# The last tile's expert outputs: one load for both halves, summed by TensorE, and a norm that reads PSUM

## The reference

```python
def _rmsnorm(x, g):
    xf = x.astype(jnp.float32)
    y = xf * lax.rsqrt(jnp.mean(xf * xf, axis=-1, keepdims=True) + RMS_EPS)
    return (y * g.astype(jnp.float32)).astype(x.dtype)

    # in _hier_moe: every token gets the weighted outputs of its two experts
    for e in range(N_EXPERTS):
        hid = jax.nn.silu(t @ w_gate[e]) * (t @ w_up[e])
        out = out + combine[:, e:e + 1] * (hid @ w_down[e]).astype(jnp.float32)

    # in _layer and reference
    x = x + _hier_moe(_rmsnorm(x, g_ffn), ...)
    y_prompt = _rmsnorm(xp, g_final)
    y_sample = _rmsnorm(xs, g_final)
```

## Time and profile before

| What | Value |
|---|---|
| Time, median of 3 runs | 513.92 us (513.32 to 516.14) |
| Profiled execution | 512.16 us, its span 510.40 us |
| Mean granted clock of TensorE | 0.984 |
| Busy: TensorE, VectorE, ScalarE, GpSimd | 468.6, 295.2, 114.2, 206.4 us |
| DMA over the span | 141.35 MB, mean 277 GB/s |

### The profile page before, as it was taken

How to read it: one execution, slowest core, us unless ns; L and a number is a source line. 1 busy time by engine, 2 the same in 40 slices (tenths; PEclk the granted TensorE clock), 3 DMA queues, 4 the chain that set the end, 5 groups by cost and what they waited for, 6 DMA issues and landing times.

```text
span 510.4 us, 9147 instructions
## 1 busy us (share of the span) xinstructions
PE 468.6 (92%) x3279; PEld 279.5 (55%) x3280; DVE 295.2 (58%) x575; ACT 114.2 (22%) x231; POOL 206.4 (40%) x298
## 2 busy tenths in 40 slices
PE   6999999999999999999789989989978999897993
PEld 3887777777777734645454444434434444443431
DVE  4219999999999946556843233323223333332367
ACT  5130010110112332112422122212212211221243
POOL 3010914694769840011263443444434344434600
PEclk9989999999999999999799999999999999999997
DMA  8796004300000099869969999999999999999995
GB/s 326 245 378 149 1 3 171 158 1 0 1 0 1 1 308 414 310 223 327 401 257 412 382 399 405 411 367 412 409 405 408 409 415 410 413 403 410 400 335 198
DMA packets 47571, 141.35 MB, mean 277 GB/s; under 512 B 10338, under 2 KB 12402, under 8 KB 43435
## 3 DMA queue, kind: packets, MB, share of 16 engines
q1 hardware_dynamic: 41466, 128.80, 66.3%
q0 software_dynamic: 4960, 9.49, 5.0%
q10 hardware_dynamic: 1113, 2.62, 1.3%
HBM read 134.90 MB, written 13.19 MB: 290 GB/s over the span
## 4 chain that ended last, share of the span: by engine, by line
PE 71%; DMA 7%; SPq 7%; DVE 6%; POOL 3%; issue 3%; ACT 2%; DVEq 0%; ACTq 0%; POOLq 0%
PE banks L1557 26%; PE banks L1774 10%; PE banks L1794 9%; PE banks L1769 8%; PE banks L1615 8%; DMA region_x<-in_w_up 3%; DMA region_w<-in_w_in 3%; SPq L488 2%; SPq L494 2%; PE banks L1865 2%; PE banks L1784 2%; PE banks L1721 1%; DVE region_m L1431 1%; DVE region_m L1429 1%; PE banks L1645 1%
## 5 line engine op out<-in xcount | busy, mean ns | idle before, releaser
L1557 PE MATMUL banks<-region_m,region_w 128*128 128x256 f32 (+1 forms) x576 | 141.9, 410 | 0.0
L1557 PEld LDWEIGHTS banks<-region_m,region_w 128*128 128x128 f32 x576 | 110.7, 192 | 30.4 <-issue 0.4
L1418 DVE TENSOR_TENSOR region_m<-region_m,banks 128x512 f32<-128x512 f32 x30 | 20.6, 688 | 71.7 <-ACT region_m L787 71.7
L1089 DVE SCALAR_TENSOR_TENSOR z<-region_m,z 128x512 f32<-128x512 f32 x60 | 49.6, 826 | 0.0
L950 POOL COPY scol<-sidx 128x1 uint32 x28 | 13.4, 480 | 86.8 <-DVE region_m L1418 86.8
L1429 DVE TENSOR_TENSOR region_m<-region_m,banks 128x128 f32<-128x128 f32 x30 | 8.7, 288 | 65.5 <-ACT region_m L781 65.5
L1089 DVE SCALAR_TENSOR_TENSOR region_x<-region_m,region_x 128x512 f32<-128x512 f32 x56 | 45.5, 812 | 0.0
L863 POOL TENSOR_TENSOR region_m<-region_x 128x512 f32<-128x512 f32 x4 | 20.2, 5046 | 61.4 <-ACT region_m L666 30.8
L1794 PE MATMUL banks<-region_w,region_m 128*32 128x512 f32 x272 | 40.3, 598 | 2.8 <-DVE region_m L1431 2.8
L787 ACT ACTIVATE region_m<-banks,w_row 128x512 f32<-128x512 f32 x30 | 20.6, 687 | 97.6 <-PE banks L1794 97.6
L654 ACT ACTIVATE region_x<-banks 128x256 f32<-128x256 f32 (+1 forms) x40 | 14.2, 407 | 120.7 <-PE banks L1557 103.9
(11 more groups left out here) (265 smaller groups left out, 723.0 us busy)
## 6 DMA issues: line engine op xcount, KB each, us to landing
region_w<-in_w_down SPq DMA_DIRECT2D x16, 1024.0 KB, 16.0
region_w<-in_w_gate SPq DMA_DIRECT2D x12, 1024.0 KB, 13.1
region_w<-in_w_up SPq DMA_DIRECT2D x12, 1024.0 KB, 16.0
region_m<-in_w_down SPq DMA_DIRECT2D x12, 1024.0 KB, 17.6
region_w<-in_w_in SPq DMA_DIRECT2D x4, 2048.0 KB, 15.2
region_m<-in_w_gate SPq DMA_DIRECT2D x8, 1024.0 KB, 14.8
region_m<-in_w_up SPq DMA_DIRECT2D x8, 1024.0 KB, 17.2
region_w<-in_w_out SPq DMA_DIRECT2D x1, 4096.0 KB, 12.9
```

The costliest lines, as they stand in the source:

```text
L1089: last[j % 2] = conv(nc.vector.scalar_tensor_tensor(out=acc[j % 2], in0=ub[:, c, j:j + SEQ], scalar=wB(c, j), in1=acc[j % 2], op0=ALU.mult ...
L1418: nc.vector.tensor_tensor(yblk[b], yblk[b], held[b], ALU.add).then_inc(s_ya, 1)
L1557: ins = mm(ps[2 * bank + j][:, 0:LEN[j]], sec[name][:, k, c * P:(c + 1) * P], hT[:, k, CUT[j]], start=(k == 0), stop=(k == KC - 1))
```

## The change

FINISH becomes (0, 1, 2, 3, 4), and the samples' tile stands last. Its two y, 64 rows each, are no longer loaded to partitions 0 to 63 of two buffers by two transfers, but by one transfer to all 128 partitions of one buffer (ysam): the first expert's rows to partitions 0 to 63, the second's to 64 to 127. TensorE adds both into the tile's bank with one more pair of products, whose other operand (both_halves) has two ones in each column. GpSimd makes it by adding the two halves of the identity. VectorE's additions both(4) and total(4) go. ScalarE's square and VectorE's norm of this tile read PSUM. The additions of tiles 2 and 3 on TensorE (add_y) follow each tile's last_y.

```diff
-BY_PE, BY_DVE = (2, 3), (0, 1, 4)
-FINISH = (0, 1, 4, 2, 3)
+BY_PE, BY_DVE = (2, 3), (0, 1)
+FINISH = (0, 1, 2, 3, 4)
...
+        ysam = yg[0][NT - 1]
+        both_halves = token[:, 0:T]
...
-        sums = {t: banks[:, i * 512:(i + 2) * 512] for t, i in zip(FINISH, (0, 4, 0, 6, 2))}
+        sums = {t: banks[:, i * 512:(i + 2) * 512] for t, i in zip(FINISH, (0, 4, 6, 2, 0))}
...
             for t in FINISH:
+                if t == NT - 1:
+                    sp.dma_start(ysam[:, :],
+                                 y_dram.rearrange("(k n) d -> k n d", n=NTOK)[0:2, t * P:t * P + TROWS[t], :]).then_inc(s_ysam, 16)
+                    continue
                 for k in range(2):
                     sp.dma_start(yg[k][t][0:TROWS[t], :], y_dram[k * NTOK + t * P:k * NTOK + t * P + TROWS[t], :])\
                       .then_inc(s_yg[k][t], 16)
...
-                act.wait_ge(s_fin, at + 1)
-                nc.scalar.activation(yg[0][t][0:n, :], xf[0:n, t, :], ACT.Square,
+                if t == NT - 1:
+                    act.wait_ge(s_comb, NT)
+                    of = sums[t]
+                else:
+                    act.wait_ge(s_fin, at + 1)
+                    of = xf[:, t, :]
+                nc.scalar.activation(yg[0][t][0:n, :], of[0:n, :], ACT.Square,
...
+            pool.wait_ge(s_ohl, 2)
+            pool.tensor_tensor(both_halves, ident[:, 0:T], ident[:, T:P], ALU.add).then_inc(s_ohl, 1)
...
-                    nc.vector.scalar_tensor_tensor(out=xf[0:n, t, cut], in0=xf[0:n, t, cut], scalar=c, in1=gfin[0:n, cut],
+                    of = sums[t][0:n, cut] if t == NT - 1 else xf[0:n, t, cut]
+                    nc.vector.scalar_tensor_tensor(out=xf[0:n, t, cut], in0=of, scalar=c, in1=gfin[0:n, cut],
...
-            both(4)
             dve.wait_ge(s_gfin, 16)
             normed(0)
-            total(4)
+            total(2)
             normed(1)
-            total(2)
-            normed(4)
             total(3)
             normed(2)
             normed(3)
+            normed(4)
...
-            pe.wait_ge(s_ohl, 2)
+            pe.wait_ge(s_ohl, 3)
...
+            last_y(0).then_inc(s_comb, 1)
+            last_y(1).then_inc(s_comb, 1)
+            last_y(2)
+            add_y(2).then_inc(s_comb, 1)
+            last_y(3)
+            add_y(3).then_inc(s_comb, 1)
+
+            pe.wait_ge(s_fin, 1)
+            last_y(4)
+            pe.wait_ge(s_ysam, 16)
+            n = TROWS[4]
+            for j in range(2):
+                ins = mm(sums[4][0:n, j * 512:(j + 1) * 512], both_halves, ysam[:, j * 512:(j + 1) * 512],
+                         start=False, stop=True)
+            ins.then_inc(s_comb, 1)
```

More of the change, by code:

```diff
@@ L336, in build_step @@
         s_wexp = [[sem(f"s_wexp{i}_{n}") for n in ("gate", "up", "down")] for i in range(NSLOT)]
-        s_yg = [[sem(f"s_yg{k}_{t}") for t in range(NT)] for k in range(2)]
+        s_yg = [[sem(f"s_yg{k}_{t}") for t in range(NT - 1)] for k in range(2)]
+        s_ysam = sem("s_ysam")
         s_sq3 = sem("s_sq3")
@@ L1867, in last_y, with add_y @@
                 return ins
[L1870 to L1877, removed]
+            def add_y(t):
                 pe.wait_ge(s_yg[0][t], 16)
@@ L1881, in _ @@
                              start=False, stop=True)
-                ins.then_inc(s_comb, 1)
+                return ins
+            last_y(0).then_inc(s_comb, 1)
[12 more added lines that the diff above has]
+            ins.then_inc(s_comb, 1)
 _INS = ["x_prompt", "x_sample", "state_conv_a", "state_conv_b", "g_mix", "w_in", "conv_a_w", "conv_b_w",
```

## The result

The changed kernel takes 517.90 us (median; 516.67 to 518.87), against 513.92 (513.32 to 516.14). The ratio is 1.0067, with a 95% interval from 1.0051 to 1.0083: slower by 3.4 us (the medians differ by 3.98), and the whole interval lies above the 0.5% that the prediction called measurable. The prediction had the direction, the mechanism and a range that holds it (516.6 to 522.0), but said 520.1; the forecast's own, narrower range (518.8 to 521.8) doesn't hold it.

What follows compares the result with a forecast made beforehand. The prediction took the samples' load on two DMA engines as the bound: landing 506.7 + 0.05 + additions 3.9 + tail 5.98 = 516.6 us, 6.2 over 510.40, so 513.92 + 6.2 = 520.1 us; range 516.6 to 522.0.

Steps and rivals of the forecast that it cites:

- the mechanism: Samples' y load: its outermost count of 2 leaves two DMA engines, so 262,144 bytes each take 10.4 us.
- the forecast's own, narrower range: Kernel time 518.8 to 521.8 us, for two engines and half clock; chance 0.58.
- TensorE's own work: TensorE at the end: ready for the samples' additions at 502.3 us; with their load there, done at 504.2.
- the changes of form: TensorE switching between 64-row and full products: 0.20 us each, five in place of one, 0.7 us more taken.
- The landing: The samples' y load, last of nine: lands at 506.2 to 507.2 us, taken as 506.7.
- The wait: TensorE ahead of the last additions: stands from 502.3 to 506.7 us, 4.4 us, for the samples' load.
- The clock: TensorE's last additions run at granted clock 0.50 after the wait: 3.9 us, against 1.99 at full level.
- rival A: Samples' load on two engines but TensorE at full clock, additions 1.99 us: 518.2 us, chance 0.22.
- The tail of 5.98 us: From the last product's end through square, reciprocal, norm and stores to the end: 0.11 + 1.51 + 4.36 us.
- The wide range: Kernel time 516.6 to 522.0 us, taking in two engines with full clock and an early landing.
- Rival B: Samples' load over all 16 engines, landing at 498.1 us and hidden: 513.7 us, not slower, chance 0.14.
- VectorE's work: Two VectorE additions for tile 4 go, up to 2.4 us, but the last product then sets the end.

Runs made afterwards that it cites:

- the counts of 2 and 4: Count 2 is the changed kernel's load, 517.90 us; count 4 replaces it by two 64-row loads, each source written 4 x 16 x 1024: 513.89 us, ratio 1.0002.
- TensorE kept busy: The changed kernel plus ten bf16 products into an unread bank ahead of TensorE's wait for the samples' load: 517.83 us, ratio 1.0063.
- The kernel with pairs: The changed kernel, its one samples' load written with outermost count 64 (row n of both experts on partitions 2n and 2n+1), identity matched: 513.72 us, ratio 0.9982.
- the fastest kernel here: The changed kernel with the samples' load at outermost count 64 and tile 2's two y added by VectorE, not TensorE: 513.72 us, ratio 0.9950.

## Why the prediction was right, and where its sizes were off

- **The mechanism.** The step on which all rested, from the store with a count of 8 and 49.8% to two engines for a count of 2, came out: a share of 0.12 to 0.13, and the loss goes when the outermost count is 64. The step rested on one row that allowed a second reading (an even split between two queues), so that it held was not certain from rows 7; the counts of 2 and 4 show it.
- **TensorE's own work.** Predicted to be ready for the last additions at S + 13.2 (502.3 − 489.13), measured 13.0. With the load hidden, its last pass ends at S + 14.89, predicted 15.07. The term of the changes of form was a little too large: 0.7 us, measured 14.89 − 12.63 − 1.72 = 0.54. The price of one change behind it, 0.20 us, isn't borne out as a constant (0.20, 0.10 and 0 in three comparisons).
- **The landing.** This is the term that was off most. Predicted S + 17.6 (506.7), measured 507.17 − 491.64 = S + 15.5. At 53 GB/s, 524,288 bytes take 9.9 us, where I had 10.4. The rest, 1.6 us, is the start, by an estimate from that rate: 507.17 − 9.9 = 497.3, 1.8 us before the eighth load landed at 499.1. The window from 498 to 499 bears it out: the share is 0.18 there, so most of the 16 engines had no work left, while the eighth had not landed. I had started the ninth at the eighth's landing (496.3, S + 7.2; by the estimate S + 5.6).
- **The wait** followed: 2.54 us, not 4.4, where the prediction asked for 4 us or more. The load landed 18.56 us behind its issue, where it asked for over 19. The predicted sign that did show was the two engines busy alone.
- **The clock.** Forecast at the half level for all four passes (3.9 us), with the full level as rival A (2.0). It was between: 3.12 us. The mean of 0.90 from 507 to 508 puts the fall at 507.8, 3.1 us after the stop (504.67) and 0.6 us into the passes. With TensorE kept busy they took 1.93. Before, it fell 2.8 us after the stop; with the load issued first, 5.2 us.
- **The tail of 5.98 us** behind the last product: 516.30 − 510.33 = 5.97. That the last stores are smaller saved nothing.
- **The sum.** −2.1 for the landing, −0.8 for the clock: 6.2 − 2.9 = 3.3, measured 3.39. Both misses point the same way. The measured 517.90 lies 0.3 us from rival A's 518.2 and under the forecast's own range, but neither of A's terms (a landing at S + 17.6, the full clock throughout) is what happened; that it is so near is chance. The wide range holds the result because its lower end was set for A.
- **Rival B**, the load over all engines, was put at 513.7 us, 0.2 under before. The kernel with pairs has a ratio of 0.9982, 0.9 us under (0.2 to 1.7 by the interval). Its tail is 0.42 us shorter than before's: the 0.2 that was named, and 0.2 less for the changes of form (15.07 − 14.89).
- **VectorE's work.** Removing its two additions for tile 4 gave next to nothing while TensorE's chain was the longer one (a ratio of 0.9982), as said; the chain could be rebalanced only by giving one back, which is the fastest kernel here.

## What to carry to other kernels

Merging two transfers into one can cost more than it saves when the merged access pattern begins with a small dimension: 512 KB took about 10 us on two engines, while with the 64 rows outermost the same bytes landed 1.3 us behind the load before. Write the large dimension first and arrange the partitions to match; here it cost a different identity matrix. And what stands in the queue behind such a transfer needs the same engines and is late too, so issuing it earlier can be worse (13.8 us here). When a step leaves the busiest engine, look at which chain is then the longest, and move work back to the engine that now waits.

## What the runs showed that I had not expected

- With the load of two engines issued first, all engines together moved 252 GB/s at a share of 1.04, against 408 at 1.01 before; the cause is open.
- SP's issue of a 512 KB load took up to 2.3 us, against 0.45, while the two engines were behind.
- S lies between 489.1 and 493.8 us in ten profiles, which is more than the effects here; between before and changed, 2.38 of the 2.51 us are there by the middle of the kernel. Times of the end must be read from S, and the ratio of the runs from many of them.
